# A hybrid mixer layer on one core: the first branch's operand is split beside the query projections, its passes ride in every latent attention pair, and the gate rows' chain is cut into pieces

## The chip, the core and the metric

The kernel runs on one core of a Trainium2 chip. The metric is the device time of that core in microseconds (us). TensorE (PE) multiplies, its weight loads (PEld) overlap its matmuls, VectorE (DVE) and ScalarE (ACT) work through their own programs in order, SyncE (SP) issues the transfers. GpSimd does next to nothing here.

## The reference, cut to what matters

One trunk layer is run for 128 context tokens and 512 latent tokens with the same weights: a half-step SwiGLU FFN, a token mixer, a second FFN. Shapes: D_MODEL 1024, 8 mLSTM heads (64 x 128), 16 query heads over 4 key heads of 64, 128 cached keys.

```python
mq, mk, mv, mo, mg, aq, ak, av, bg = jnp.split(h @ w_in, idx, axis=-1)
hm, C, n, m = mlstm_bidir(mq, mk, mv, mg, C0, n0, m0)     # gates mg: log i, log f, both directions
hm = rms_norm(hm, m_norm) * sigmoid(mo)                   # first branch's operand
ha = block_attention(aq, k_all, v_all)                    # second branch's operand
g = jax.nn.sigmoid(bg.reshape(B, T, 2, D_MODEL))
y = g[:, :, 0] * (hm @ w_bm) + g[:, :, 1] * (ha @ w_ba)
return y @ w_out
```

Context queries see the 128 context keys alone; latent queries see 512 latent and 128 cached keys in one softmax. Everything is float32.

## The kernel before, in words

Activations lie feature-major: 8 chunks of 128 features by 640 tokens (128 context, then 512 latent). A projection tile is 128 output features. Its weights (128 x 1024) are split by ACT into a rounded high part (`whi`, `split` at L850) and by DVE into the rest (`wlo`, L1178); the activations are split in the same way (`_hi`, `_lo`). A tile is 8 chunks x 2 halves of 320 tokens x 3 products (hi*hi, hi*lo, lo*hi): 48 matmuls, 24 for each half (`project`, L446 to 464). Splits run two tiles ahead of PE: `split(t.plus(2))`, into two slots.

Every engine has its own program; the order of work is written out by hand, and semaphores tie the programs together. The mixer's tiles are numbered l: L_GATE (0), four L_MQ (1 to 4), four L_MK (5 to 8), eight L_MV, then output gates and branch gates, L_AV, L_AK, eight L_AQ (queries), and the projections L_BM (first branch), L_BA (second branch) and L_OUT.

Three places are touched.

1. The gate rows. Tile 0 gives 8-partition rows of the gates (`gi`, `gf`). DVE and ACT turn them into stabilised log sums: `forget` (L1392), ACT's Exp and Ln (L992, L994), DVE's `scans` (a step, ten cumulative sums, four maximum scans, small copies, four row operations; L1394 to L1430), ACT's four exponentials (L997 to L1000), then PE's `turn_gates` (transposes and small products, L605, L608) and DVE's `take_gates`. Before the change, DVE runs `forget` at l = 0 and all of `scans` at l = 1, behind the split of tile 3 and ahead of the split of tile 4; ACT's four exponentials stand at l = L_MK - 1 and PE's `turn_gates` behind tile L_MK, where each later tile is followed by one `turn` (a transpose of an earlier tile).

2. The first branch's operand. `out_gate` (L1550) multiplies `hm` by its gate, one chunk for each query tile. The split of `hm` is ACT's `high` (L1109) and DVE's `low_m` (L1614). Both stand in the first eight attention pairs.

3. The attention pairs. A pair is one block of 128 queries for two heads. There are 32 latent pairs (block c >= 1, 640 keys) and 8 context pairs (c = 0, 128 keys). `ORDER` lists them: eight latent pairs, and then eight groups of three latent pairs and one context pair. For pair k, PE runs the scores of pair k + 1 (L756, L759; L751 for context), the transposes of pair k's probabilities (`turn_p`, L775), from the ninth pair on one `fill`, and `values` (L785). A `fill` is a quarter of an L_BM tile, 12 matmuls (L805 to L807); 32 of them do the eight tiles. DVE runs for pair k the two row maxima (`top`, L1585, ahead of the next exponentials), `take_second` of pair k - 1 (L1599, L1602: copies that `values` waits for), the two divisions, `low_ha` (L1609), and behind them what belongs to the fills: `take_fill` (L1624) and a weight split. ACT runs `take_p`, the exponentials of pair k + 1 (L1104), `high_ha` (L1096), and behind them `high`, a gate's Tanh or a weight split.

PE's order for one pair is this:

```python
for k in range(PAIRS):
    if k + 1 < PAIRS:
        scores(k + 1)
    turn_p(k)
    if k >= KC:
        fill(k - KC)
    values(k)
```

The scores of pair k + 1 wait for both exponentials of pair k (`aexp`), the transposes of pair k for `low_ha` of pair k - 1, and the maxima of pair k + 1 for its scores.

Of the kernel before, what the change touches and what calls it, by code (L numbers as in the profile page):

```python
# [21 lines left out]
P = 128  # L22
# [69 lines left out]
def build(nc, a):  # L92
    ctx = ExitStack()
    with ctx:
# [95 lines left out]
        m_hi = at("m_hi", [P, KC, N], F32R, r2)  # L190
# [255 lines left out]
        def _(pe):  # L446
# [343 lines left out]
            def fill(f):  # L790
# [35 lines left out]
            for m in range(KC):  # L826
                gemm(L_OUT + m, h_hi, h_lo, yl if m == 0 else None)
# [16 lines left out]
        def _(act):  # L844
# [28 lines left out]
            def square_y(l, m, t):  # L873
# [4 lines left out]
                fn(sq[m % 2][:, :], y[:, m, :], ACT.Square).then_inc(ysq_in, 1)  # L878
                act.wait_ge(ysq_in, KC * (l + 1) + m + 1)
                for g, cols in GROUPS:  # L880
                    last = fn(y[:, m, cols], y[:, m, cols], ACT.Copy, scale=post_s[:, l, m, g:g + 1])
# [87 lines left out]
            for l in range(L_MO):  # L969
# [20 lines left out]
                else:  # L990
# [4 lines left out]
                if l == L_MK - 1:  # L995
# [59 lines left out]

            def inv_rms(e):
# [7 lines left out]
            for l in range(L_AV, L_BM):  # L1064
# [17 lines left out]
                if l > L_AK:  # L1082
                    inv_rms(l - 1 - L_AK)

# [22 lines left out]
            def high(k, dst, src, ready, count, out):  # L1107
                act.wait_ge(ready, count)
                copy(dst[:, k, :], src).then_inc(out, 1)  # L1109

# [3 lines left out]

            exponentials(0, 0)
# [3 lines left out]
            for k in range(PAIRS):  # L1119
# [5 lines left out]
                if k < KC:  # L1125
                    high(k, h_hi, hm[:, k, :], mg, k + 1, mg_hi)
                elif k % 4 == 0:
                    gate_of(KC + (k - KC) // 4)
                elif k % 4 == 3:
                    split(Tile(T_MIX + L_BM + (k - KC) // 4 + 2))  # L1130

            for l in range(L_BA, L_OUT):
# [5 lines left out]
                if m >= 1:  # L1138
                    high(m - 1, h_hi, y[:, m - 1, :], y_sum, m, yh)
            act.preload_act_table_set(LN_EXP)  # L1140
            high(KC - 1, h_hi, y[:, KC - 1, :], y_sum, KC, yh)

            for l in range(L_OUT, L_END):
# [4 lines left out]
                copy(halves(y[:, m, :]), both(t.slot)).then_inc(ev[t.slot], 1)  # L1148
# [18 lines left out]
        def _(dve):  # L1167
# [42 lines left out]
            def residual(l):  # L1210
# [3 lines left out]
                for k in range(KC):  # L1214
# [3 lines left out]
                    tt(sa[k % 2][:, :], y[:, k, :], rb[:, :], ALU.mult).then_inc(post_t, 1)  # L1218
# [175 lines left out]
            def scans():  # L1394
                dve.wait_ge(row_a, 2)
                row_step(stt(gf[:, :, :], gf[:, :, :], 0.0, t1[:, :, :], ALU.min, ALU.subtract))
                for c in range(NT):
                    for d in range(2):
                        seg = slice(c * P, (c + 1) * P) if d == 0 else slice((c + 1) * P - 1, c * P - 1 if c else None, -1)
                        row_step(dve.tensor_tensor_scan(gb[:, d, seg], one_row, gf[:, d, seg], 0.0, ALU.mult, ALU.add), False)  # L1400
                for d in range(2):
                    for g, cols in GROUPS:
                        if d:
                            cols = slice(cols.stop - 1, cols.start - 1 if cols.start else None, -1)
                        row_step(dve.tensor_tensor_scan(gm[:, d, cols], gf[:, d, cols], gi[:, d, cols],
                                                        m0[:, d:d + 1] if g else 0.0, ALU.add, ALU.max), False)
                dve.wait_ge(row_d, rows[0])
                row_step(dve.memset(m_in[:, :, 0:1], 0.0), False)
                row_step(copy(m_in[:, 0, 1:2], m0[:, 0:1]), False)
                row_step(copy(m_in[:, 1, NT - 1:NT], m0[:, 1:2]), False)  # L1410
                row_step(copy(m_in[:, 0, 2:NT], gm[:, 0, 2 * P - 1:(NT - 1) * P:P]), False)
                row_step(copy(m_in[:, 1, 1:NT - 1], gm[:, 1, 2 * P:(NT - 1) * P + 1:P]), False)
                row_step(copy(mout[:, 0:1], gm[:, 0, TP - 1:TP]), False)
                row_step(copy(mout[:, 1:2], gm[:, 1, 0:1]), False)
                assert rows[0] == ROW_M
                row_step(tt(gi[:, :, :], gi[:, :, :], gb[:, :, :], ALU.subtract), False)
                row_step(tt(nm[:, :, :], gb[:, :, :], gm[:, :, :], ALU.subtract))
                row_step(copy(nml[:, 0, :], nm[:, 0, P - 1:N:P]), False)
                row_step(copy(nml[:, 1, :], nm[:, 1, 0:N:P]))

                def tiles(v):
# [359 lines left out]
```

## Time and profile before

| | |
|---|---|
| three runs | 1950.55, 1951.1, 1955.57 us; median 1951.1 |
| the profiled execution | 1955.21 us, span 1953.4 us |
| PE busy | 1844.7 us (94%) |
| PEld / DVE / ACT busy | 1764.6 (90%) / 940.2 (48%) / 651.6 (33%) us |
| mean granted PE clock | 0.977 |
| HBM | 90 GB/s over the span |

The span is what the profiler records from the first to the last instruction; the 1.8 us beside it lie around it. A busy share is an average over the whole span; the places named above make up about 50 us (gate rows) and 225 us (attention pairs) of it. A granted clock of 1.00 is 2.4 GHz, 0.50 is 1.2 GHz.

### The profile page before, as it was taken

The page shows a single profiled execution, that of the slowest core. Times are in us where ns is not written, and L with a number is a line of the kernel's source. Part 1 is how long each engine was busy: PE and PEld are TensorE (multiplying, and loading weights), DVE is VectorE, ACT ScalarE, POOL GpSimd, SP SyncE. Part 2 cuts the span into 40 slices and gives each one's busy share as a digit, 9 for nine tenths or more (in the row PEclk, how much of TensorE's full clock was granted, in tenths as well). Part 3 has the DMA queues.
Part 4 walks back from the last instruction along what each step waited for, and adds up shares of the span by engine and source line. Part 5 has one row for each costly group of instructions (what it writes and reads, how often), then busy time and mean ns, then how long its engine had stood idle before and what let it go on. Part 6 is the DMA issues. An engine that isn't in the chain of part 4 may idle for free.

```text
span 1953.4 us, 31481 instructions
## 1 busy us (share of the span) xinstructions
PE 1844.7 (94%) x12888; PEld 1764.6 (90%) x12888; DVE 940.2 (48%) x1578; ACT 651.6 (33%) x1067; POOL 0.2 (0%) x4
## 2 busy tenths in 40 slices
PE   6999999999978999999999789999979999999996
PEld 6999999999958998899999668889959999999996
DVE  4665465642575224444434787774363222222235
ACT  3422222112354222533334454442463222221233
POOL 0000000000000000000000000000000000000000
PEclk9999999999988999999999899999989999999997
DMA  7454444412431224222332201112302222222221
GB/s 297 147 159 130 139 150 130 151 65 83 140 100 47 64 74 99 84 75 71 89 123 73 87 2 54 36 36 83 130 33 67 75 74 75 75 75 76 73 57 54
DMA packets 52294, 178.38 MB, mean 91 GB/s; under 512 B 8521, under 2 KB 11099, under 8 KB 51427
## 3 DMA queue, kind: packets, MB, share of 16 engines
q1 hardware_dynamic: 52195, 176.97, 28.1%
q8 instruction: 72, 1.18, 0.2%
q14 instruction: 27, 0.22, 0.0%
HBM read 162.40 MB, written 13.90 MB: 90 GB/s over the span
## 4 chain that ended last, share of the span: by engine, by line
PE 83%; DVE 9%; ACT 4%; issue 3%; DMA 0%; SPq 0%; DVEq 0%; ACTq 0%
PE psum L461 23%; PE psum L462 22%; PE psum L463 22%; PE psum L785 2%; PE psum L503 2%; DVE amax L1585 1%; PE psum L775 1%; PE psum L492 1%; PE psum L756 1%; PE psum L675 1%; DVE x L1213 1%; PE psum L648 1%; DVE macc L1242 1%; DVE wlo L1178 1%; ACT whi L850 1%
## 5 line engine op out<-in xcount | busy, mean ns | idle before, releaser
L461 PE MATMUL psum<-h_hi,whi 128*128 128x320 f32 x2288 | 719.0, 314 | 9.0 <-DVE wlo L1178 7.5
L462 PE MATMUL psum<-h_lo,whi 128*128 128x320 f32 x2288 | 708.9, 310 | 0.0
L463 PE MATMUL psum<-h_hi,wlo 128*128 128x320 f32 x2288 | 708.8, 310 | 0.0
L1178 DVE TENSOR_TENSOR wlo<-raw,whi 128x1024 fp32r<-128x1024 f32 x213 | 260.7, 1225 | 799.7 <-ACT whi L850 798.6
L461 PEld LDWEIGHTS psum<-h_hi,whi 128*128 128x128 f32 x2288 | 431.7, 189 | 15.6 <-DVE wlo L1178 7.8
L462 PEld LDWEIGHTS psum<-h_lo,whi 128*128 128x128 f32 x2288 | 431.8, 189 | 1.9 <-issue 1.9
L463 PEld LDWEIGHTS psum<-h_hi,wlo 128*128 128x128 f32 x2288 | 431.4, 189 | 0.0
L850 ACT CAST whi<-raw 128x1024 fp32r<-128x1024 f32 x213 | 222.3, 1044 | 380.3 <-PE psum L463 370.1
L461 PE MATMUL psum<-g_hi,whi 128*128 128x320 f32 x704 | 218.3, 310 | 1.2 <-DVE g_lo L1307 1.2
L462 PE MATMUL psum<-g_lo,whi 128*128 128x320 f32 x704 | 217.6, 309 | 0.0
L463 PE MATMUL psum<-g_hi,wlo 128*128 128x320 f32 x704 | 217.5, 309 | 0.0
L1242 DVE SCALAR_TENSOR_TENSOR macc<-mw,silc,macc 128x512 f32<-128x512 f32 x210 | 142.7, 744 | 0.0
L461 PEld LDWEIGHTS psum<-g_hi,whi 128*128 128x128 f32 x704 | 132.3, 188 | 1.7 <-DVE g_lo L1307 1.7
L462 PEld LDWEIGHTS psum<-g_lo,whi 128*128 128x128 f32 x704 | 132.3, 188 | 0.0
L463 PEld LDWEIGHTS psum<-g_hi,wlo 128*128 128x128 f32 x704 | 132.3, 188 | 0.0
L928 ACT ACTIVATE sa<-psum 128x640 f32<-128x640 f32 x44 | 31.0, 705 | 151.4 <-PE psum L463 148.4
L785 PE MATMUL psum<-sb,av 128*64 128x128 f32 x672 | 46.6, 282 | 20.5 <-DVE sb L1602 20.4
L785 PEld LDWEIGHTS psum<-sb,av 128*64 128x64 f32 x672 | 37.3, 139 | 28.9 <-issue 28.9
L934 ACT CAST g_hi<-sb 128x640 f32 x44 | 32.1, 729 | 93.2 <-DVE sb L1301 93.2
L1104 ACT ACTIVATE sa<-psum,amax 128x640 f32<-128x640 f32 (+1 forms) x80 | 56.1, 709 | 12.3 <-DVE amax L1585 12.3
L1585 DVE TENSOR_REDUCE amax<-psum 128x1 f32<-128x640 f32 (+1 forms) x80 | 53.5, 710 | 11.2 <-PE psum L759 11.1
L1307 DVE TENSOR_TENSOR g_lo<-sb,g_hi 128x640 f32 x44 | 36.2, 823 | 36.8 <-ACT g_hi L934 36.8
(218 smaller groups left out, 1978.2 us busy)
## 6 DMA issues: line engine op xcount, KB each, us to landing
raw<-in_w_ffn_in SPq DMA_DIRECT2D x88, 512.0 KB, 3.5
raw<-in_w_mix SPq DMA_DIRECT2D x77, 512.0 KB, 3.8
mw<-in_w_mod SPq DMA_DIRECT2D x28, 768.0 KB, 4.7
raw<-in_w_ffn_out SPq DMA_DIRECT2D x32, 512.0 KB, 3.6
mw<-in_w_mod SPq DMA_DIRECT2D x4, 2048.0 KB, 19.6
gate<-gate_keep SPq DMA_DIRECT2D x24, 320.0 KB, 4.9
mw<-in_w_mod SPq DMA_DIRECT2D x14, 512.0 KB, 3.6
gate_keep<-gate SPq DMA_DIRECT2D x20, 320.0 KB, 4.6
```

Of the source, the lines that this page charges most:

```text
L461: mm(out, whi[t.slot][:, k, :], hi[:, k, cols], start=(k == 0), stop=False)
L462: mm(out, whi[t.slot][:, k, :], lo[:, k, cols], start=False, stop=False)
L463: last = mm(out, wlo[t.slot][:, k, :], hi[:, k, cols], start=False, stop=(k == nk - 1))
L503: last = mm(mod_out(2 * t + g, bank), macc[:, g, t * P:(t + 1) * P], ones_d, start=True, stop=True)
L785: last = mm(psum[s * HD:(s + 1) * HD, T_LAST, 2 * P:3 * P], av[:, v, (m // 2) * HD:(m // 2 + 1) * HD], sb[s][:, b * P:(b + 1) * P], start= ...
L850: copy(whi[t.slot][:, :, :], raw[t.raw][:, :, :]).then_inc(w_hi, 1)
L934: copy(out, sb[s][:, :]).then_inc(g_hi_s, 1)
L1104: fn(sa[s][:, 0:w], flat(s)[:, 0:w], ACT.Exp, bias=amax[:, s:s + 1], accum_out=asum[:, s:s + 1]).then_inc(aexp, 1)
L1178: tt(wlo[t.slot][:, :, :], raw[t.raw][:, :, :], whi[t.slot][:, :, :].bitcast(F32), ALU.subtract).then_inc(raw_free, 1)
L1242: last = stt(acc, w[:, k, :], by, acc, ALU.mult, ALU.add)
L1307: tt(g_lo[:, jj, :].rearrange("p o n -> p (o n)"), sb[s][:, :], g_hi[:, jj, :].rearrange("p o n -> p (o n)").bitcast(F32), ALU.subtract).t ...
L1585: dve.tensor_reduce(amax[:, s:s + 1], flat(s)[:, 0:w], AX.X, ALU.max, negate=True).then_inc(nmx, 1)
```

## The change

- The gate rows: `forget` moves to l = 1 and ACT's Exp and Ln with it, behind that tile's copy and split. `scans` gets a part number: the first step and the ten sums at l = 2, the maximum scans and small copies at l = 3, the row operations at l = 4, each behind its tile's weight split. ACT's four exponentials, `turn_gates` and `take_gates` move one tile later (L_MK, L_MK + 1). The `turn` that stood behind tile L_MK + 1 now goes behind L_MK + 2, which has two.
- The operand: `high` and `low_m` write new tiles `a_hi` and `a_lo` (`a_lo` lies where `hm` lies) and run during the query tiles, one chunk for each, one and two tiles behind `out_gate`. What is left of them is `high` of the last chunk ahead of ACT's first exponentials, `low_m` of the last but one behind DVE's query tiles, and `low_m` of the last in pair 0. `m_hi` moves to where `h_hi` lies, and a new `yg` to where `h_lo` lies; it takes the branch sum and the output that `y` had in the mixer.
- The pairs: `ORDER` becomes eight groups of four latent pairs and one context pair. `FILL` gives each latent pair one fill and the context pairs none. DVE takes a half of a fill's tile in the iteration behind the fill; the fourth fill's half and the weight split fall in the iteration of the context pair. ACT's Tanh stands behind the second fill and its split behind the fourth. The last `take_fill` and split, which stood behind the loop, are gone from there.

```diff
-ORDER = [(1, m) for m in range(KC)]
+ORDER, FILL = [], []
 for i in range(KC):
-    ORDER += [(2 + n // KC, n % KC) for n in range(3 * i, 3 * i + 3)] + [(0, i)]
+    ORDER += [(1 + n // KC, n % KC) for n in range(4 * i, 4 * i + 4)] + [(0, i)]
+    FILL += [4 * i, 4 * i + 1, 4 * i + 2, 4 * i + 3, None]
...
-        m_hi = at("m_hi", [P, KC, N], F32R, r2)
+        a_hi = at("a_hi", [P, KC, N], F32R, r2)
+        a_lo = at("a_lo", [P, KC, N], F32R, r1)
+        m_hi = at("m_hi", [P, KC, N], F32R, h_at)
+        yg = at("yg", [P, KC, N], F32, h_at + KC * row)
...
-                if l == L_MK:
+                if l == L_MK + 1:
                     turn_gates()
-                if l > L_MK:
+                if l == L_MK + 2:
+                    turn(0)
+                if l >= L_MK + 2:
                     turn(l - L_MK - 1)
...
-                    mm(out, whi[t.slot][:, k, :], h_hi[:, k, cols], start=(k == 0), stop=False)
-                    mm(out, whi[t.slot][:, k, :], h_lo[:, k, cols], start=False, stop=False)
-                    last = mm(out, wlo[t.slot][:, k, :], h_hi[:, k, cols], start=False, stop=(k == KC - 1))
+                    mm(out, whi[t.slot][:, k, :], a_hi[:, k, cols], start=(k == 0), stop=False)
...
-                if k >= KC:
-                    fill(k - KC)
+                if FILL[k] is not None:
+                    fill(FILL[k])
...
             for m in range(KC):
                 gemm(L_BA + m, m_hi, m_lo)
             for m in range(KC):
-                gemm(L_OUT + m, h_hi, h_lo, yl if m == 0 else None)
+                gemm(L_OUT + m, a_hi, a_lo, yl if m == 0 else None)
...
                 if l > L_GATE:
                     split(t.plus(2))
-                else:
+                if l == L_GATE + 1:
                     act.wait_ge(row_d, 1)
...
-                if l == L_MK - 1:
+                if l == L_MK:
                     act.wait_ge(row_d, ROW_END)
...
+                if l > L_AQ:
+                    m = l - 1 - L_AQ
+                    high(m, a_hi, hm[:, m, :], mg, m + 1, mg_hi)
...
+            high(KC - 1, a_hi, hm[:, KC - 1, :], mg, KC, mg_hi)
             exponentials(0, 0)
...
-                if k < KC:
-                    high(k, h_hi, hm[:, k, :], mg, k + 1, mg_hi)
-                elif k % 4 == 0:
-                    gate_of(KC + (k - KC) // 4)
-                elif k % 4 == 3:
-                    split(Tile(T_MIX + L_BM + (k - KC) // 4 + 2))
+                f = FILL[k]
+                if f is not None and f % 4 == 1:
+                    gate_of(KC + f // 4)
+                if f is not None and f % 4 == 3:
+                    split(Tile(T_MIX + L_BM + f // 4 + 2))
...
-            def scans():
-                dve.wait_ge(row_a, 2)
...
+            def scans(part):
+                if part == 0:
+                    dve.wait_ge(row_a, 2)
+                    row_step(stt(gf[:, :, :], gf[:, :, :], 0.0, t1[:, :, :], ALU.min, ALU.subtract))
+                    for c in range(NT):
+                        for d in range(2):
...
+                elif part == 1:
                     for d in range(2):
-                        seg = slice(c * P, (c + 1) * P) if d == 0 else slice((c + 1) * P - 1, c * P - 1 if c else None, -1)
...
+                    assert rows[0] == ROW_M
+                else:
+                    row_step(tt(gi[:, :, :], gi[:, :, :], gb[:, :, :], ALU.subtract), False)
+                    row_step(tt(nm[:, :, :], gb[:, :, :], gm[:, :, :], ALU.subtract))
...
                 if l == 0:
                     dve.wait_ge(tile_done, 2 + T_MIX)
                     dve.memset(vt[:, :, :, DV:DV + 1], 1.0).then_inc(ones_v, 1)
+                if l == 1:
                     forget()
-                if l == 1:
-                    scans()
-                if l == L_MK:
+                if l in (2, 3, 4):
+                    scans(l - 2)
+                if l == L_MK + 1:
                     take_gates()
-                if l > L_MK:
+                if l == L_MK + 2:
+                    take_turned(0)
+                if l >= L_MK + 2:
                     take_turned(l - L_MK - 1)
...
+            def low_m(m):
+                dve.wait_ge(mg_hi, m + 1)
+                tt(a_lo[:, m, :], hm[:, m, :], a_hi[:, m, :].bitcast(F32), ALU.subtract).then_inc(mg_lo, 1)
...
+                if l > L_AQ + 1:
+                    low_m(l - 2 - L_AQ)
+            low_m(KC - 2)
...
-                if 1 <= k <= KC:
-                    low_m(k - 1)
-                if k > KC and k % 2 == 0:
-                    f = k - KC - 1
+                if k == 0:
+                    low_m(KC - 1)
+                f = FILL[k - 1] if k else None
+                if f is not None and f % 2:
                     take_fill(f // 4, f // 2 % 2)
                     if f % 4 == 3:
                         split(Tile(T_MIX + L_BM + f // 4 + 2))
             take_second(PAIRS - 1)
             low_ha(PAIRS - 1)
-            take_fill(KC - 1, 1)
-            split(Tile(T_MIX + L_BA + 1))
...
-                tt(y[:, m, :], y[:, m, :], sb[m % 2][:, :], ALU.add).then_inc(y_sum, 1)
+                tt(yg[:, m, :], yg[:, m, :], sb[m % 2][:, :], ALU.add).then_inc(y_sum, 1)
```

## Rows read from the trace of the kernel before

**Rows 1.** Page, part 4: shares of the chain that ended last, by engine

```profile
PE 83%; DVE 9%; ACT 4%; issue 3%; DMA 0%; SPq 0%; DVEq 0%; ACTq 0%
```

**Rows 2.** Waits of PE: place, releaser, us in total, times, longest

```profile
PE psum L785 <- DVE sb L1602: 20.4, 15, 1.9
...
PE psum L461 <- DVE wlo L1178: 7.5, 1, 7.5
```

**Rows 3.** Timeline of DVE, gate rows: start us, us, engine, line, operation

```profile
612.80 1.47 DVE L1416 TENSOR_TENSOR gi<-gi,gb 8x1280 f32<-8x1280 f32 x1
...
618.86 2.34 DVE L1178 TENSOR_TENSOR wlo<-raw,whi 128x1024 fp32r<-128x1024 f32 x2
```

**Rows 4.** Timeline of ACT: tile 4's copy, last of the four exponentials

```profile
630.23 0.70 ACT L979 ACTIVATE mq<-psum 128x640 f32<-128x640 f32 x1 [15.95 <-PE psum L463]
...
634.20 1.25 ACT L1000 ACTIVATE gm<-gm 8x1280 f32<-8x1280 f32 x1
```

**Rows 5.** Windows: busy us of PE, PEld, DVE, ACT, POOL; PEclk, DMA share, GB/s

```profile
981.00:983.70 2.70, 0.34 (x4) 0.10 (x2) 2.47 (x7) 0.06 (x1) 0.00 (x0) 1.00 0.11 26
984.80:988.00 3.20, 3.20 (x17) 2.98 (x14) 1.80 (x7) 1.01 (x4) 0.00 (x0) 0.50 0.48 166
...
1100.70:1111.00 10.30, 7.39 (x44) 6.15 (x45) 7.13 (x17) 4.24 (x8) 0.00 (x0) 0.50 0.24 93
1111.00:1153.00 42.00, 29.43 (x315) 25.31 (x315) 35.84 (x81) 23.49 (x53) 0.00 (x0) 1.00 0.00 1
...
620.10:626.30 6.20, 6.18 (x23) 6.19 (x24) 1.10 (x1) 0.00 (x0) 0.00 (x0) 0.50 0.50 169
626.30:630.00 3.70, 3.70 (x27) 3.70 (x26) 0.00 (x0) 0.00 (x0) 0.00 (x0) 1.00 0.00 0
```

**Rows 6.** Timelines of ACT and DVE, last query tile: idle before, releaser, in brackets

```profile
1089.38 0.79 ACT L1074 ACTIVATE aq<-psum,vT 128x640 f32<-128x640 f32 x1 [5.17 <-PE psum L463]
...
1091.74 1.23 DVE L1178 TENSOR_TENSOR wlo<-raw,whi 128x1024 fp32r<-128x1024 f32 x1 [4.22 <-ACT whi L850]
```

**Rows 7.** Timeline of DVE: a chunk's low part and the next maxima

```profile
1127.22 0.82 DVE L1614 TENSOR_TENSOR h_lo<-hm,h_hi 128x640 fp32r<-128x640 f32 x1 [0.32 <-ACT h_hi L1109]
...
1127.96 1.55 DVE L1585 TENSOR_REDUCE amax<-psum 128x1 f32<-128x640 f32 x2
```

**Rows 8.** Timeline of PE: pair 0, then values of two unfilled pairs

```profile
1102.34 2.37 PE L775 MATMUL psum<-cst,sa 128*128 128x128 f32 x10 [1.78 <-DVE sa L1592]
1105.97 2.40 PE L785 MATMUL psum<-sb,av 128*64 128x128 f32 x20 [1.27 <-DVE sb L1602]
...
1124.95 1.31 PE L785 MATMUL psum<-sb,av 128*64 128x128 f32 x20 [1.86 <-DVE sb L1602]
...
1130.65 1.31 PE L785 MATMUL psum<-sb,av 128*64 128x128 f32 x20 [1.86 <-DVE sb L1602]
```

**Rows 9.** Timeline of PE, one group of four: the values of its pairs

```profile
1216.63 1.31 PE L785 MATMUL psum<-sb,av 128*64 128x128 f32 x20 [0.94 <-DVE sb L1602]
...
1222.15 1.31 PE L785 MATMUL psum<-sb,av 128*64 128x128 f32 x20
...
1227.17 1.31 PE L785 MATMUL psum<-sb,av 128*64 128x128 f32 x20
...
1229.70 0.44 PE L775 MATMUL psum<-cst,sa 128*128 128x128 f32 x2
...
1231.82 0.44 PE L785 MATMUL psum<-sb,av 128*64 128x128 f32 x4
```

**Rows 10.** Timeline of DVE in the same group, around the context pair

```profile
1228.85 0.29 DVE L1609 SCALAR_TENSOR_TENSOR m_lo<-psum,m_hi 128x128 fp32r<-128x128 f32 x1 [1.46 <-ACT m_hi L1096]
...
1233.24 0.48 DVE L1624 SCALAR_TENSOR_TENSOR y<-gate,psum 128x320 f32<-128x320 f32 x1
...
1233.87 1.23 DVE L1178 TENSOR_TENSOR wlo<-raw,whi 128x1024 fp32r<-128x1024 f32 x1
```

**Rows 11.** The chain of work: values of the next group's first pair

```profile
1237.69 1.31 PE psum L785 x20
```

More of the change, by code:

```diff
@@ L804, in fill @@
                 for k in range(4 * part, 4 * part + 4):
-                    mm(out, whi[t.slot][:, k, :], h_hi[:, k, cols], start=(k == 0), stop=False)
-                    mm(out, whi[t.slot][:, k, :], h_lo[:, k, cols], start=False, stop=False)
-                    last = mm(out, wlo[t.slot][:, k, :], h_hi[:, k, cols], start=False, stop=(k == KC - 1))
+                    mm(out, whi[t.slot][:, k, :], a_hi[:, k, cols], start=(k == 0), stop=False)
+                    mm(out, whi[t.slot][:, k, :], a_lo[:, k, cols], start=False, stop=False)
+                    last = mm(out, wlo[t.slot][:, k, :], a_hi[:, k, cols], start=False, stop=(k == KC - 1))
                 if part == 1:
@@ L1054, in _, with high @@
             store_hm(UNITS - 2)
+            def high(k, dst, src, ready, count, out):
+                act.wait_ge(ready, count)
+                copy(dst[:, k, :], src).then_inc(out, 1)
             def inv_rms(e):
@@ L1147, in _ @@
                 act.wait_ge(yl, m + 1)
[L1148 removed]
+                copy(halves(yg[:, m, :]), both(t.slot)).then_inc(ev[t.slot], 1)
                 if l == L_END - 1:
@@ L1392, in forget @@
                 row_step(stt(t1[:, :, :], gf[:, :, :], -1.0, gf[:, :, :], ALU.mult, ALU.max))
-            def scans():
-                dve.wait_ge(row_a, 2)
-                row_step(stt(gf[:, :, :], gf[:, :, :], 0.0, t1[:, :, :], ALU.min, ALU.subtract))
-                for c in range(NT):
-                    for d in range(2):
-                        seg = slice(c * P, (c + 1) * P) if d == 0 else slice((c + 1) * P - 1, c * P - 1 if c else None, -1)
[L1400 to L1421, printed above, removed]
-                    return v[:, :, :].rearrange("h d (c t) -> h (d c) t", t=P)
-                def spread(v):
-                    return v[:, :, :].rearrange("h d (c o) -> h (d c) o", o=1).broadcast_to([H, 2 * NT, P])
-                row_step(tt(ar[:, :, :], m_in[:, :, :], nml[:, :, :], ALU.add), False)
-                row_step(tt(tiles(t1), tiles(nm), spread(m_in), ALU.add), False)
-                row_step(tt(tiles(gf), tiles(gi), spread(nml), ALU.add), False)
-                assert rows[0] == ROW_END
@@ new lines, in tiles, with spread @@
+            def tiles(v):
+                return v[:, :, :].rearrange("h d (c t) -> h (d c) t", t=P)
+            def spread(v):
+                return v[:, :, :].rearrange("h d (c o) -> h (d c) o", o=1).broadcast_to([H, 2 * NT, P])
+            def scans(part):
[4 more added lines that the diff above has]
+                        for d in range(2):
+                            seg = slice(c * P, (c + 1) * P) if d == 0 else slice((c + 1) * P - 1, c * P - 1 if c else None, -1)
+                            row_step(dve.tensor_tensor_scan(gb[:, d, seg], one_row, gf[:, d, seg], 0.0, ALU.mult, ALU.add), False)
+                elif part == 1:
+                    for d in range(2):
+                        for g, cols in GROUPS:
+                            if d:
+                                cols = slice(cols.stop - 1, cols.start - 1 if cols.start else None, -1)
+                            row_step(dve.tensor_tensor_scan(gm[:, d, cols], gf[:, d, cols], gi[:, d, cols],
+                                                            m0[:, d:d + 1] if g else 0.0, ALU.add, ALU.max), False)
+                    dve.wait_ge(row_d, rows[0])
+                    row_step(dve.memset(m_in[:, :, 0:1], 0.0), False)
+                    row_step(copy(m_in[:, 0, 1:2], m0[:, 0:1]), False)
+                    row_step(copy(m_in[:, 1, NT - 1:NT], m0[:, 1:2]), False)
+                    row_step(copy(m_in[:, 0, 2:NT], gm[:, 0, 2 * P - 1:(NT - 1) * P:P]), False)
+                    row_step(copy(m_in[:, 1, 1:NT - 1], gm[:, 1, 2 * P:(NT - 1) * P + 1:P]), False)
+                    row_step(copy(mout[:, 0:1], gm[:, 0, TP - 1:TP]), False)
+                    row_step(copy(mout[:, 1:2], gm[:, 1, 0:1]), False)
+                    assert rows[0] == ROW_M
+                else:
+                    row_step(tt(gi[:, :, :], gi[:, :, :], gb[:, :, :], ALU.subtract), False)
+                    row_step(tt(nm[:, :, :], gb[:, :, :], gm[:, :, :], ALU.subtract))
+                    row_step(copy(nml[:, 0, :], nm[:, 0, P - 1:N:P]), False)
+                    row_step(copy(nml[:, 1, :], nm[:, 1, 0:N:P]))
+                    row_step(tt(ar[:, :, :], m_in[:, :, :], nml[:, :, :], ALU.add), False)
+                    row_step(tt(tiles(t1), tiles(nm), spread(m_in), ALU.add), False)
+                    row_step(tt(tiles(gf), tiles(gi), spread(nml), ALU.add), False)
+                    assert rows[0] == ROW_END
```

23 lines of the change are left out of this document (9 added, 14 removed).

## The prediction, made before the change was built

> **What bounds the kernel now.** I read the chain of waits first: 83% of what ended last is PE [rows 1]. So a change pays only where PE stands idle or runs at the lower of its two clock levels. The list of PE's waits names the places that this change can reach [rows 2]: 7.5 us once, in front of a projection tile that waits for the low part of its weights (DVE, L1178), and 20.4 us in 15 waits for DVE's copies ahead of `values`. Then I went to the timelines of these stages, and to the windows for the granted clock. The reader is to see two things. DVE runs its program in order, so the weight split of tile 4 stands behind the whole chain of the gate rows and starts only at 618.86 [rows 3]. And in the attention pairs PE is idle 1.86 us in each pair without a fill [rows 8], while the filled latent pairs of a group have at most 0.94 [rows 9].
>
> **The gate rows in pieces.** Removed is the wait of 7.5 us [rows 2]. With it goes a stretch at 1.2 GHz that it left behind: from 620.1 to 626.3 PE was busy throughout at clock 0.50 and started 23 matmuls in 6.2 us; right behind it, at 1.00, it started 27 in 3.7 us [rows 5]. At the second rate the 23 take 3.2 us, so 3.0 us were lost. Together 10.5 us.
>
> Is something late next? A tile costs PE about 7.0 us (tile 4 from 620.1 to its copy at 630.23 is 10.1, less the 3.0 lost [rows 4, 5]). The largest piece is the row operations, 612.80 to 618.86, 6.1 us [rows 3]. Behind the end of a tile come ACT's copy and split (0.7 and about 1.05, the split taken from the gap up to the exponentials), DVE's split 1.2, hence 3.0 with the hand-overs, and then the piece: 9.1 us behind the end of tile 4, or 2.1 behind the end of tile 5. ACT's exponentials follow; copy, split and exponentials took 630.23 to 635.45, 5.2 us, of which the exponentials are some 3.5 [rows 4]. They end 5.6 us behind tile 5, and `turn_gates` is not reached before 7.0. Slack 1.4 us, so no new wait: 0, with up to 4 us if the pieces queue worse than this. `turn_gates` itself only changes place. The two moved turns and the later `o_m` transfer have nobody waiting. I take -10.5; the ends are -7.5 (the clock is low there for another cause) and -12.
>
> **The operand's split in the query tiles.** ACT waits 5.17 us for PE in each query tile, DVE 4.22 us for ACT [rows 6]; one `high` and one `low_m` (0.74 us from start to start [rows 7]) fit in, price 0. At the end the cover is gone: the last two `low_m` stand in DVE's queue ahead of the first row maximum, on which ACT's exponentials and PE's scores wait. 2 x 0.74 = +1.5. The last `low_m` falls in pair 0 and delays its maxima by 0.74, but PE then has a fill in front of `values`. In pair 0 the fill's 12 matmuls at the low clock (6.2/23 = 0.27 us each) are 3.2 us in place of an idle 1.27 [rows 8]: +1.9. Against that, the three steps from 1105.97 to 1124.95 took 19.0 us instead of 3 x 5.70 = 17.1, because the low clock lasted until 1111 [rows 5, 8]; a PE without idle should have the high clock back by the start of `values`: -1.9. Sum of this part +1.5, ends 0 and +4.
>
> **Passes in each latent pair.** Steps are counted from one `values` to the next. Before: eight unfilled pairs of 5.70 [rows 8] and eight groups of 1237.69 - 1216.63 = 21.06 [rows 9, 11]: 214.1 us. After, a group of five:
> - two steps from latent to latent, PE without idle: 5.52 each, and 5.02 for the one whose scores are the short context scores [rows 9];
> - the step into the context pair. It has no fill now, and DVE has `take_fill` and a weight split there, ahead of the next pair's maxima, and only behind these the small copy that the context's `values` need. From `values`: 1.68 to `low_ha`, 0.29, 0.63 for `take_fill` until the split, 1.23 split, 1.55 for two maxima [rows 7, 9, 10], about 0.3 for the copy (as the 0.29 of the other 128-wide operation), less small overlaps: 5.6. Before it was 4.65 [rows 9];
> - the step out of the context pair: 5.87 before, of which 0.94 was idle behind the same DVE split [rows 9, 11]; the split is gone from there: 4.93.
>
> Sum 5.52 + 5.52 + 5.02 + 5.6 + 4.93 = 26.6, eight times 212.8: -1.3 us. So 17 us of idle in the unfilled pairs are filled, and nearly all of it comes back in the context pairs. Ends -4 and +3.
>
> **The clock in the context pairs.** The new idle is in one piece. Behind `values` PE has the next scores and the two small transposes until 1229.70 + 0.44, 2.97 us behind 1227.17 [rows 9]; then nothing until 5.6: 2.6 us idle, 0.44 of `values`, and again a short wait. What does the clock do with this? At 981 PE was idle for 2.4 us (0.34 busy in 2.70), and from 984.8 to 988.0 the clock stood at 0.50, with PE busy throughout. In the unfilled pairs, with 1.86 us idle each, it stayed at 1.00 from 1111 to 1153 [rows 5, 8]. The new idle is beyond the one that cost the clock. One such fall costs 3.2 us at half speed, 1.5 us by the rate above; a long one, as at 620.1, 3.0 us. Seven context pairs have work behind them. The ends are no fall, 0, and seven long ones, 21 us. I take five short ones, since the idle is only a little beyond the nearest row, and the place of a fall varied: +7.5.
>
> The Trainium skill (TensorE: Matmul & The Clock Gate, Part 1) has PE fall to 1.2 GHz once it has been idle for a while. Read strictly, an idleness that `values` interrupts does not count, no context pair would lose the clock, and the sum would lack the 7.5. By that rule this case's trace differs: at 981 the idle stretch was 2.4 us, PE was busy again at once, and the clock fell all the same [rows 5].
>
> **The sum.** -10.5 + 1.5 - 1.3 + 7.5 = -2.8 us. On the profiled execution's own time, 1955.2 (span 1953.4 and 1.8 around it), that is 1952.4. That execution lies 4.1 above the median of the three runs, 1951.1, so the forecast for the median is 1948.3.
>
> **The rivals.**
> - The clock holds in the context pairs. For it: the stretch is broken by `values`, and the unfilled pairs kept the clock with 30% idle. Against it: 2.6 is more than 2.4. Then -10.3: 1940.8.
> - It ends slower, by one mechanism: the idle in front of each context pair's `values` takes the clock all seven times, and for long stretches as at 620.1, at 3.0 each: 21 us against 10.3 gained, +10.7: 1961.8. It decides from a mean of 1.5 us for each of the seven. For it: the low clock at 1100.7 lasted 10.3 us with PE only 72% busy [rows 5]. Against it: behind a context pair come fills without idle, and behind 984.8 it lasted 3.2.
> - The gate rows' wait goes only in half, because the pieces queue behind splits that wait for ACT: 3.7 us stay and the clock still falls. Then -3.8 in place of -10.5: +3.9, 1955.0. Against it: the slack of 1.4 us above.
>
> **How the numbers follow.** Forecast (three to seven falls near 1.5) 0.57, the clock holds 0.25, all long 0.13, half the wait 0.05. The forecast's own range is 1945.3 (three falls) to 1951.3 (seven). The range for 8 in 10 takes in the first rival nearly and the third: 1941 to 1955. About 0.3%, 5.9 us, is what a measurement of this kernel can tell from no change. Faster by more: the first rival, and the part of the forecast with three falls or fewer, 0.25 + 0.13 = 0.38. Slower by more: most of the second rival, some of the third, and spread, 0.16. Within: 0.46.
>
> **What would show it.** In the profile after: no idle of PE ahead of tile 4, `wlo` of tile 4 ready some 4 us early, and clock 1.00 from 613 on until `turn_gates`; the first maximum 1.5 us behind the last `hm` product; every latent step at 5.5 or 5.0; `values` of a context pair with 2.6 us idle in front, released by DVE's copy; clock 0.50 behind most context pairs. Wrong would be a context step under 5 us (then the maxima don't stand behind the split), a clock of 1.00 through the pairs (first rival), or a wait at `turn_gates` for ACT (third).

## The result, and the profile after

Median 1958.2 us (1955.36 to 1959.43, 8 runs), against 1953.3 us for the kernel before on the same chip (1950.33 to 1955.57, 8 runs). The ratio is 1.0026, 95% interval 1.0018 to 1.0035: 4.9 us slower, inside the 0.3% that I had called no change, and outside my range of 1941 to 1955.

| | before | after |
|---|---|---|
| median of the runs, us | 1953.3 | 1958.2 |
| profiled execution, us | 1955.2 | 1957.5 |
| its span, us | 1953.4 | 1955.8 |
| granted clock, mean | 0.977 | 0.973 |
| PE in the chain that ended last | 83% | 87% |
| waits for DVE's copy ahead of `values` | 15, 20.4 us | 8, 20.4 us |

The share of PE in the chain rose and so did the time: the chain now passes through PE where it passed through DVE (9% before, 6% now), and PE itself is busy 8.5 us longer (1853.2 against 1844.7). A larger share of PE is no gain by itself. Here are the chain's shares in part 4 of the page:

```profile
PE 87%; DVE 6%; ACT 4%; issue 2%; DMA 0%; SPq 0%; DVEq 0%; ACTq 0%
```

and PE's waits (place, releaser, us in total, times, longest). The wait for `wlo` of [rows 2] is gone from the list. The 20.4 us for DVE's copy are the same sum in half as many pieces, which are longer, seven of 2.67 and the eighth of 1.72:

```profile
PE psum L791 <- DVE sb L1621: 20.4, 8, 2.7
```

**The gate rows.** DVE's timeline (start, us, engine, line, operation, idle before and its releaser in brackets) now alternates row operations and splits. `wlo` of tile 4 is made at 605.64; before, DVE reached that split at 618.86 [rows 3]:

```profile
605.64 1.23 DVE L1188 TENSOR_TENSOR wlo<-raw,whi 128x1024 fp32r<-128x1024 f32 x1 [4.50 <-ACT whi L856]
606.78 1.47 DVE L1413 SCALAR_TENSOR_TENSOR gf<-gf,t 8x1280 f32<-8x1280 f32 x1
...
619.65 1.23 DVE L1188 TENSOR_TENSOR wlo<-raw,whi 128x1024 fp32r<-128x1024 f32 x1 [2.33 <-ACT whi L856]
620.79 1.47 DVE L1435 TENSOR_TENSOR gi<-gi,gb 8x1280 f32<-8x1280 f32 x1
```

**The pairs.** PE's timeline: the scores of pair 1, then the steps around the second context pair, then the first tile behind the pairs. A step is counted from one `values` (L791) to the next: 5.01 into the last latent pair of the group, 5.64 into the context pair, 6.35 out of it:

```profile
1088.58 1.70 PE L762 MATMUL psum<-ak,aq 64*128 64x256 f32 x8 [4.79 <-ACT sa L1118]
...
1096.81 1.31 PE L791 MATMUL psum<-sb,av 128*64 128x128 f32 x20
...
1136.15 1.31 PE L791 MATMUL psum<-sb,av 128*64 128x128 f32 x20
1141.16 1.31 PE L791 MATMUL psum<-sb,av 128*64 128x128 f32 x20
1143.69 0.44 PE L781 MATMUL psum<-cst,sa 128*128 128x128 f32 x2
1146.80 0.51 PE L791 MATMUL psum<-sb,av 128*64 128x128 f32 x4 [2.67 <-DVE sb L1621]
...
1153.15 1.31 PE L791 MATMUL psum<-sb,av 128*64 128x128 f32 x20
...
1317.53 0.51 PE L465 MATMUL psum<-m_hi,whi 128*128 128x320 f32 x1 [0.69 <-DVE m_lo L1631]
```

The reader is to see the idle of 2.67 in one piece, and what DVE does meanwhile. Its timeline has the weight split and two maxima, and the copy that PE waits for at their end:

```profile
1143.77 1.23 DVE L1188 TENSOR_TENSOR wlo<-raw,whi 128x1024 fp32r<-128x1024 f32 x1 [0.25 <-ACT whi L856]
1144.91 1.54 DVE L1607 TENSOR_REDUCE amax<-psum 128x1 f32<-128x640 f32 x2
1146.37 0.28 DVE L1621 COPY sb<-psum 128x128 f32<-128x128 f32 x1
```

**The clock.** The windows have the columns of [rows 5]; the column behind POOL is the granted clock:

```profile
596.00:640.00 44.00, 44.00 (x309) 43.78 (x308) 23.18 (x38) 16.16 (x18) 0.00 (x0) 0.96 0.23 79
634.00:638.00 4.00, 4.00 (x21) 3.98 (x21) 1.42 (x3) 0.00 (x0) 0.00 (x0) 0.63 0.38 135
1100.00:1318.00 218.00, 193.09 (x1728) 167.68 (x1727) 153.50 (x392) 96.97 (x247) 0.00 (x0) 0.93 0.09 30
1147.00:1149.80 2.80, 2.63 (x16) 1.86 (x12) 1.34 (x4) 0.62 (x3) 0.00 (x0) 0.51 0.50 196
1149.80:1174.00 24.20, 22.10 (x212) 19.48 (x210) 17.73 (x45) 10.87 (x28) 0.00 (x0) 0.99 0.01 2
1174.50:1180.40 5.90, 5.55 (x27) 4.63 (x28) 3.40 (x10) 2.33 (x7) 0.00 (x0) 0.50 0.39 132
1317.30:1320.70 3.40, 3.17 (x12) 3.17 (x13) 0.18 (x1) 0.48 (x1) 0.00 (x0) 0.56 0.62 236
```

Over all eight groups the clock is 0.93, where the long quiet stretch of before had 1.00 [rows 5]. It falls behind every one of the eight context pairs, back to full within the same group. Six of these stretches are about 3.4 us long, and two, at the third and the sixth context pair, about twice that; the one at 1147 is the second, the one of 1174.5 to 1180.4 the third. The eighth lies in the first tile behind the pairs, at 1317.

The chain gives the length of a group. It has the `values` of the fourth latent pair of the first group and of the eighth, seven groups later:

```profile
1112.95 1.27 PE psum L791 x20
...
1312.30 1.27 PE psum L791 x20
```

(1312.30 - 1112.95) / 7 = 28.48 us, where the prediction has 26.6 without falls. That is 1.9 us a group.

### The profile page after: what moved, and what is told of

Same layout as the page of the kernel before. It is cut to its first block, busy times and chain, and to the rows that moved or that the text cites. A ratio compares the mean times of both kernels' runs of the same rounds, so it can differ in the third digit from the quotient of the medians.

```text
span 1955.8 us, 31481 instructions
## 1 busy us (share of the span) xinstructions
PE 1853.2 (95%) x12888; PEld 1771.7 (91%) x12888; DVE 941.0 (48%) x1578; ACT 650.5 (33%) x1067; POOL 0.2 (0%) x4
## 4 chain that ended last, share of the span: by engine, by line
PE 87%; DVE 6%; ACT 4%; issue 2%; DMA 0%; SPq 0%; DVEq 0%; ACTq 0%
PE psum L465 23%; PE psum L467 22%; PE psum L466 22%; PE psum L781 2%; PE psum L791 2%; PE psum L762 2%; PE psum L507 1%; PE psum L496 1%; PE psum L811 1%; PE psum L812 1%; PE psum L813 1%; ACT whi L856 1%; PE psum L681 1%; DVE x L1223 1%; PE psum L654 1%
## 5 line engine op out<-in xcount | busy, mean ns | idle before, releaser
L465 PE MATMUL psum<-h_hi,whi 128*128 128x320 f32 x2160 | 678.1, 314 | 1.5 <-ACT gate L1018 1.5
L466 PE MATMUL psum<-h_lo,whi 128*128 128x320 f32 x2160 | 668.4, 309 | 0.0
L467 PE MATMUL psum<-h_hi,wlo 128*128 128x320 f32 x2160 | 668.3, 309 | 0.0
L465 PEld LDWEIGHTS psum<-h_hi,whi 128*128 128x128 f32 x2160 | 406.5, 188 | 7.8 <-issue 5.4
L466 PEld LDWEIGHTS psum<-h_lo,whi 128*128 128x128 f32 x2160 | 406.7, 188 | 1.9 <-issue 1.9
L467 PEld LDWEIGHTS psum<-h_hi,wlo 128*128 128x128 f32 x2160 | 406.5, 188 | 0.0
L791 PE MATMUL psum<-sb,av 128*64 128x128 f32 x672 | 46.4, 281 | 20.4 <-DVE sb L1621 20.4
L791 PEld LDWEIGHTS psum<-sb,av 128*64 128x64 f32 x672 | 36.4, 138 | 28.3 <-issue 28.3
L1607 DVE TENSOR_REDUCE amax<-psum 128x1 f32<-128x640 f32 (+1 forms) x80 | 53.5, 710 | 16.1 <-PE psum L765 16.1
L781 PE MATMUL psum<-cst,sa 128*128 128x128 f32 x336 | 51.2, 302 | 4.3 <-DVE m_lo L1631 3.0
```

The lines of the kernel that those rows point to most:

```text
L465: mm(out, whi[t.slot][:, k, :], hi[:, k, cols], start=(k == 0), stop=False)
L466: mm(out, whi[t.slot][:, k, :], lo[:, k, cols], start=False, stop=False)
L467: last = mm(out, wlo[t.slot][:, k, :], hi[:, k, cols], start=False, stop=(k == nk - 1))
L781: last = tp(turned(s, b), sa[s][:, b * P:(b + 1) * P], ident)
L791: last = mm(psum[s * HD:(s + 1) * HD, T_LAST, 2 * P:3 * P], av[:, v, (m // 2) * HD:(m // 2 + 1) * HD], sb[s][:, b * P:(b + 1) * P], start= ...
L1607: dve.tensor_reduce(amax[:, s:s + 1], flat(s)[:, 0:w], AX.X, ALU.max, negate=True).then_inc(nmx, 1)
```

## The experiments

All times are medians of four or five runs, each beside the kernel before on the same chip: 1953.1 us for the first four experiments, 1953.5 for the next four, 1952.8 for the last three.

### Each half by itself

The gate rows alone, on the kernel before:

```
 for l in range(2, L_MO):
     gemm(l)
-    if l == L_MK:
+    if l == L_MK + 1:
         turn_gates()
...
-    scans()
+    if l in (2, 3, 4):
+        scans(l - 2)
...
```

> The kernel before with the gate rows alone in pieces. My theory (the gate rows gain what was forecast, and the attention pairs give it back through the clock): 10.5 us faster than before, about 1943, no idle of PE ahead of tile 4. Rival (the pieces gain less than the profile says, because the profiled run of before was a slow one): 3 to 6 us faster.

The pairs alone: the changed kernel, with the gate rows as before.

> The changed kernel with the gate rows as they were before: the operand's split and the passes alone. My theory: about 15 us slower than before, 1968, of which 1.5 is low_m ahead of the first maxima and 13 to 15 the low clock behind eight context pairs. Rival (the two parts interact, for instance through where the clock's falls lie): the sum of this and the rows alone is off the changed kernel's +5 by more than 3 us.

Measured: 1942.5 us (1942.35 to 1943.03), ratio 0.9948 [0.9935, 0.9962], for the rows; 1966.2 us (1964.58 to 1969.37), ratio 1.0070 [1.0056, 1.0083], for the pairs. So -10.6 and +13.1. The sum, +2.5, is 2.4 us off the +4.9 of both together, and each of the two ratios is uncertain by about 2.6 us, so no interaction of the halves can be told. Windows of the rows' kernel: PE has no idle, and the pairs keep the clock.

```profile
596.00:640.00 44.00, 44.00 (x309) 43.78 (x308) 23.18 (x38) 16.20 (x18) 0.00 (x0) 0.96 0.22 74
1098.00:1316.00 218.00, 194.29 (x1826) 171.40 (x1825) 161.61 (x402) 104.38 (x256) 0.00 (x0) 1.00 0.10 34
```

Windows of the pairs' kernel: the same 44 us have 7.5 us of idle again, and the pairs stand at 0.93.

```profile
596.00:640.00 44.00, 36.50 (x253) 36.02 (x252) 21.95 (x37) 15.15 (x17) 0.00 (x0) 0.92 0.19 61
1108.00:1327.00 219.00, 194.10 (x1739) 168.56 (x1736) 154.03 (x392) 96.84 (x247) 0.00 (x0) 0.93 0.09 29
```

The prediction's first term, -10.5, holds. The error is in the pairs, which with the operand's split were forecast at +7.7.

### The idle filled with work that nobody reads

If the pairs cost because the clock falls, then extra matmuls in the idle should make the kernel faster:

```
 if FILL[k] is not None:
     fill(FILL[k])
+else:
+    for n in range(NWARM):      # NWARM = 24
+        mm(psum[:, T_LAST, 3 * P:4 * P], a_hi[:, n % KC, 0:P], a_hi[:, n % KC, 0:P], start=True, stop=True)
 values(k)
```

> The changed kernel with 24 extra 128-column matmuls in each context pair, between its transposes and its values, into a free quarter of a PSUM bank (nothing reads them): work added, in PE's idle 2.7 us. If the clock is the cause: clock 1.00 through the pairs, steps out of a context pair back at 4.9 us, 12 to 15 us faster than the changed kernel, about 1944. If the loss is the wait itself (DVE's chain) and the clock only goes along: the same time as the changed kernel, or up to 3 us slower.

Measured: 1944.0 us (1943.31 to 1946.11), ratio 0.9957 [0.9944, 0.9971], 14.2 us under the changed kernel. The window over the pairs, with 274 more matmul records in the same 218 us (192 of them the added ones), stands at 1.00:

```profile
1100.00:1318.00 218.00, 212.46 (x2002) 190.65 (x2001) 155.62 (x395) 98.15 (x249) 0.00 (x0) 1.00 0.10 35
```

PE's timeline of one group. The 24 matmuls take 2.88 us of the old idle, and the step out of the context pair is 1229.93 - 1224.97 = 4.96, where the changed kernel has 6.35:

```profile
1203.27 1.31 PE L792 MATMUL psum<-sb,av 128*64 128x128 f32 x20
...
1219.34 1.31 PE L792 MATMUL psum<-sb,av 128*64 128x128 f32 x20
1222.06 2.88 PE L831 MATMUL psum<-a_hi 128*128 128x128 f32 x24
1224.97 0.44 PE L792 MATMUL psum<-sb,av 128*64 128x128 f32 x4
...
1229.93 1.31 PE L792 MATMUL psum<-sb,av 128*64 128x128 f32 x20
```

The group is 1229.93 - 1203.27 = 26.66, the prediction's 26.6. So the steps were right, and 14.2 us is the price of the falls: shown, since the only change was added work. The rival, that the wait itself costs the time and the clock only goes along, is out: the step into the context pair is as long as before (1224.97 - 1219.34 = 5.63), and the 14.2 us are gone.

### The idle made shorter: the split one pair later

```
 if f is not None and f % 2:
     take_fill(f // 4, f // 2 % 2)
-    if f % 4 == 3:
-        split(Tile(T_MIX + L_BM + f // 4 + 2))
+f = FILL[k - 2] if k >= 2 else None
+if f is not None and f % 4 == 3:
+    split(Tile(T_MIX + L_BM + f // 4 + 2))
...
 low_ha(PAIRS - 1)
+split(Tile(T_MIX + L_BA + 1))
```

> The changed kernel with one thing moved: DVE's weight split stands one iteration later, behind the first latent pair of the next group. Theory: the context pair's values then wait only about 1.5 us, the step into it is 4.5 us in place of 5.6, no fall of the clock; 5 us of steps and 13 to 15 us of clock: 18 to 20 us faster than the changed kernel, about 1939, and faster than before. Rival (the split only shifts the idle into the next step, whose maxima it then delays): the idle and the falls move there, the time stays within 3 us of the changed kernel.

Measured: 1944.3 us (1942.04 to 1944.44), ratio 0.9952 [0.9939, 0.9966]. It is 13.9 under the changed kernel, but 5 us over what I expected, and this is the miss that taught most. The idle in front of the context pair's `values` is 1.58 us now (0.55 at the eighth), less than the 1.86 of the unfilled pairs that kept the clock [rows 8]. PE's timeline, at the first, the fifth and the eighth context pair:

```profile
1116.95 0.44 PE L791 MATMUL psum<-sb,av 128*64 128x128 f32 x4 [1.58 <-DVE sb L1621]
...
1219.93 1.31 PE L791 MATMUL psum<-sb,av 128*64 128x128 f32 x20
...
1224.47 0.44 PE L791 MATMUL psum<-sb,av 128*64 128x128 f32 x4 [1.58 <-DVE sb L1621]
...
1303.21 0.44 PE L791 MATMUL psum<-sb,av 128*64 128x128 f32 x4 [0.55 <-DVE sb L1621]
```

The step is 4.54 in place of 5.64. But the clock still falls, behind the second to the sixth context pair and behind the eighth; behind the first and the seventh, with the same 1.58 us of idle, it holds. The windows of this kernel: over all pairs 0.95, behind the first context pair full speed, behind the second half speed with PE busy throughout:

```profile
1100.00:1318.00 218.00, 200.49 (x1804) 177.00 (x1803) 155.22 (x394) 98.17 (x249) 0.00 (x0) 0.95 0.10 34
...
1117.40:1122.30 4.90, 4.36 (x35) 3.91 (x35) 4.81 (x12) 2.59 (x8) 0.00 (x0) 1.00 0.32 95
...
1144.20:1147.60 3.40, 3.40 (x21) 3.01 (x17) 2.97 (x5) 0.74 (x2) 0.00 (x0) 0.50 0.27 72
```

The 1.1 us that the step into the context pair lost came back in part: the moved split makes the step out of it 5.34 with 0.31 idle where the clock holds, against 4.96 before. That leaves 0.7 us for each of seven groups and 1.2 at the eighth, about 6 of the 13.9 us. The rest is in the falls: six short ones are left, at about 1.2 us each (a step out of 6.55 in place of 5.34), of the six short and two long ones. The length of PE's idle by itself doesn't tell whether the clock falls.

### The same with twelve idle matmuls

> The kernel with DVE's split one iteration later, and 12 extra 128-column matmuls in each context pair's remaining idle of 1.6 us (nothing reads them). The run with the split moved alone lost the clock behind seven of eight context pairs although its idle is shorter than the 1.86 us that the unfilled pairs of before had. Theory (the idle's length alone was the wrong measure: the small products of a context pair count for little, and real work in the gap keeps the clock): no fall in the pairs, 8 to 11 us faster than with the split moved alone, about 1935. Rival (the clock falls for the wait as such, whatever is put in): the falls stay, 1944.

The expectation counts seven falls in the kernel before this one; its profile has six. The edit is the two above together, with `NWARM = 12`. Measured: 1937.9 us (1937.28 to 1939.32), ratio 0.9919 [0.9905, 0.9932], 6.5 us under the kernel without them, where I had expected 8 to 11. The window:

```profile
1110.00:1300.00 190.00, 181.22 (x1742) 160.06 (x1738) 143.61 (x371) 91.19 (x233) 0.00 (x0) 1.00 0.09 33
```

No fall is left, and six falls cost 6.5 us, 1.1 each. The rival, that the clock falls for the wait as such, whatever is put into it, is out.

### The order of before, with the rest of the change

```
-    ORDER += [(1 + n // KC, n % KC) for n in range(4 * i, 4 * i + 4)] + [(0, i)]
-    FILL += [4 * i, 4 * i + 1, 4 * i + 2, 4 * i + 3, None]
+    ORDER += [(2 + n // KC, n % KC) for n in range(3 * i, 3 * i + 3)] + [(0, i)]
+FILL = [None] * KC + list(range(4 * KC))
...
 low_ha(PAIRS - 1)
+take_fill(KC - 1, 1)
+split(Tile(T_MIX + L_BA + 1))
```

> The changed kernel with ORDER and the fills as they were before: gate rows in pieces and the operand's split in the query tiles, but eight unfilled pairs first. It tells the two parts of the attention change apart. Theory (the order alone brings the loss; the moved split is worth 8 x 0.36 us in the unfilled pairs less 1.5 at their start): 1 to 2 us faster than the gate rows alone, about 1941, no falls in the pairs. Rival (the moved split is part of the loss, by delaying the start or by other falls): 3 us or more slower than the gate rows alone.

Measured: 1941.9 us (1941.15 to 1944.05), ratio 0.9941 [0.9927, 0.9955]. The kernel with the gate rows alone has the ratio 0.9948, so the operand's split in the query tiles, which is all that is between the two, makes no difference that can be told. The window of the pairs is at full clock:

```profile
1110.00:1300.00 190.00, 172.59 (x1652) 151.15 (x1648) 144.05 (x368) 90.90 (x231) 0.00 (x0) 1.00 0.10 33
```

The loss is thus in the order of the pairs and their fills.

### A part of the tile in the context pair

The same four parts of a tile, one of them moved from a latent pair into the context pair. The last `take_fill` and split stand behind the loop again, since the last fill now stands in the last pair:

```
-    FILL += [4 * i, 4 * i + 1, 4 * i + 2, 4 * i + 3, None]
+    FILL += [4 * i, 4 * i + 1, 4 * i + 2, None, 4 * i + 3]
...
 low_ha(PAIRS - 1)
+take_fill(KC - 1, 1)
+split(Tile(T_MIX + L_BA + 1))
```

> The changed kernel with the fourth quarter of each tile moved from the fourth latent pair into the context pair, so that a latent pair is without a fill instead (its scores are the short context ones). The split and take_fill then fall behind the next group's first pair, as before the change. Theory: the work of 1.95 us covers the context pair's wait and keeps the clock; steps 5.5, 5.5, about 4.3, 4.65, 5.9, 25.9 a group against 28.3 with the falls: 14 to 20 us faster than the changed kernel, about 1940. Rival (the idle then stands in the unfilled latent pair and takes the clock there): within 5 us of the changed kernel.

Measured: 1941.1 us (1938.68 to 1941.38), ratio 0.9933 [0.9920, 0.9947], 17.2 us under the changed kernel by one changed list, as expected. PE's timeline, with an idle of 1.27 now in front of a latent pair:

```profile
1190.26 1.31 PE L791 MATMUL psum<-sb,av 128*64 128x128 f32 x20 [1.27 <-DVE sb L1624]
```

The clock holds there too, so the rival, that the falls move with the idle, is out. The window:

```profile
1110.00:1300.00 190.00, 169.15 (x1625) 147.41 (x1623) 142.96 (x367) 91.01 (x233) 0.00 (x0) 1.00 0.10 33
```

### The tile in five parts

No pair without a fill: the 48 matmuls of a tile in parts of 12, 12, 9, 9 and 6.

```
-    FILL += [4 * i, 4 * i + 1, 4 * i + 2, 4 * i + 3, None]
+    FILL += [(i, 0, 0, 4), (i, 0, 4, 8), (i, 1, 0, 3), (i, 1, 3, 6), (i, 1, 6, 8)]
...
-                for k in range(4 * part, 4 * part + 4):
+                for k in range(lo, hi):
...
```

> The changed kernel with each L_BM tile cut into five parts of 12, 12, 9, 9 and 6 matmuls, one for every pair of a group, the context pair too; take_fill and the split of a tile fall behind the next group's first pair. Theory: no pair is without projection work, so the clock stays; steps 5.5, 5.5, 5.3, 4.6, about 4.7, 5.9: 25.6 to 26.2 a group, 16 to 20 us faster than the changed kernel, about 1940. Rival (6 matmuls, 0.9 us, are too little work for the clock): falls behind most context pairs as with the split moved alone, about 1946.

Measured: 1937.5 us (1936.35 to 1938.67), ratio 0.9916 [0.9903, 0.9930]. PE's timeline, a context pair and the latent pair behind it; the two longest idles of a group are 0.70 and 0.95:

```profile
1196.20 0.44 PE L791 MATMUL psum<-sb,av 128*64 128x128 f32 x4 [0.70 <-DVE sb L1621]
...
1202.18 1.31 PE L791 MATMUL psum<-sb,av 128*64 128x128 f32 x20 [0.95 <-DVE sb L1624]
```

Its window shows the full clock:

```profile
1110.00:1300.00 190.00, 171.78 (x1644) 149.24 (x1639) 143.93 (x372) 90.90 (x234) 0.00 (x0) 1.00 0.10 33
```

### Five parts and the split one pair later

The last part is done in the context pair, so DVE's weight split falls into the step behind it. The edit is that of the later split, on top of the five parts.

> The five-part kernel with DVE's weight split one iteration later still, behind the second latent pair. In the five-part kernel the step out of a context pair is 5.98 us with 0.95 idle, because take_fill and the split stand ahead of the next maxima. Theory: that wait shrinks to about 0.3 and the split's 1.2 us fit mostly behind a step that PE bounds: 0.4 to 0.7 us a group, 3 to 5 us faster, about 1934. Rival (the split then delays the maxima of the second step by as much): 1937, no change.

Measured: 1932.0 us (1931.38 to 1933.18, 4 runs), ratio 0.9895 [0.9880, 0.9910]. That is 5.5 us under the five parts alone, a little more than the 3 to 5 expected. The step out of the context pair is 1199.18 - 1194.22 = 4.96, without idle, where it was 5.98; the step behind it took 0.2 of this back (5.70 in place of 5.52):

```profile
1194.22 0.44 PE L791 MATMUL psum<-sb,av 128*64 128x128 f32 x4 [0.70 <-DVE sb L1621]
1199.18 1.31 PE L791 MATMUL psum<-sb,av 128*64 128x128 f32 x20
```

### The two low parts behind the first maxima

The 1.5 us that I had put on the two `low_m` ahead of the first row maximum:

```
-    if l > L_AQ + 1:
+    if L_AQ + 1 < l < L_BM - 1:
         low_m(l - 2 - L_AQ)
-low_m(KC - 2)
...
+    low_m(KC - 3)
     turn_halves(QK - 1)
...
 if k == 0:
+    low_m(KC - 2)
     low_m(KC - 1)
```

> The five-part kernel with the two low_m that stood ahead of the first maxima moved behind them: one ahead of the last key rotation, one behind pair 0's divisions. It prices the +1.5 us of the forecast by itself. Theory: the first exponentials start 1.5 us earlier, and 1.0 to 1.5 us of it reach the end: 1936.3, with the first maxima directly behind the last product with hm. Rival (pair 0's copies are then late by as much): no change, 1937.5.

And with the later split:

> Both of these together. If they are independent, the sum of the two: 1932 to 1934, the fastest of all kernels here. If either only shifts a wait, the better of the two.

Measured: 1937.9 us (1934.40 to 1938.77), ratio 0.9922 [0.9908, 0.9935], against 0.9916 for five parts alone: nothing that the medians can tell, where I had expected 1.0 to 1.5 us. PE's wait for the first exponentials is back from 4.79 to 3.31. PE's timelines, from the last rotation of the queries (L717), the kernel in five parts first, then the one with the low parts behind:

```profile
1083.13 1.31 PE L717 MATMUL psum<-sq,cst 128*128 128x320 f32 x4 [1.14 <-DVE sb L1577]
...
1090.09 2.08 PE L762 MATMUL psum<-ak,aq 64*128 64x256 f32 x8 [4.79 <-ACT sa L1118]
...
1098.11 1.31 PE L791 MATMUL psum<-sb,av 128*64 128x128 f32 x20
```

```profile
1083.99 1.31 PE L717 MATMUL psum<-sq,cst 128*128 128x320 f32 x4 [1.14 <-DVE sb L1577]
...
1089.47 1.13 PE L762 MATMUL psum<-ak,aq 64*128 64x256 f32 x8 [3.31 <-ACT sa L1118]
...
1098.26 1.31 PE L791 MATMUL psum<-sb,av 128*64 128x128 f32 x20
```

The two executions reach the rotation at different times, so the distance from it counts: the first `values` stand 14.98 us behind it in the first and 14.27 in the second. Of the 1.5 us, 0.7 arrive. The rest went in two places behind the scores: PE waits 1.95 us for DVE's divisions ahead of the turn of pair 0, where it waited 0.99, and then the fill lies deeper in the stretch of low clock that both kernels have here (to 1098.1 in place of 1096.9). A gain of 0.7 us is within the spread of these runs. The kernel with both edits measured 1930.7 us (1930.34 to 1931.95, 4 runs), ratio 0.9891 [0.9876, 0.9906]: the fastest of all, a little under the 1932 to 1934 expected, 22.1 us under the kernel before and 27.5 under the changed one, but not to be told from the 1932.0 without this edit.

## Why the prediction was wrong

It was wrong by one term, the clock's price. The forecast was -2.8 us and +4.9 was measured; the other 2.2 us between 1948.3 and 1958.2 are its base, which was the median of three runs of the kernel before (1951.1), where eight gave 1953.3. By its own steps, in the two profiled executions:

**The gate rows, -10.5: right.** From the start of tile 2 to the scores of pair 1 the kernel after is 8.9 us shorter, which holds the 1.5 that the two `low_m` add. The experiment with this half alone gives -10.6. No wait took its place, and the 1.4 us of slack at `turn_gates` held: PE is busy 44.00 of 44 us.

**The operand's split, +1.5: right in sum.** PE's wait for the first exponentials went from 3.31 to 4.79 us. Of the rest, `values` of pair 0 stand 1.5 us farther behind the scores (I had 1.9), and the next three steps take 1112.88 - 1096.81 = 16.1 us, at full clock, in place of 19.0, which holds the forecast 1.9 of low clock. Together +1.1.

**The steps, 26.6 a group: right.** Predicted 5.52, 5.52, 5.02, 5.6 and 4.93; measured 5.52, 5.52, 5.01 and 5.64 in the changed kernel and 4.96 where the clock holds; a group of 26.66.

**The clock, "I take five short ones, since the idle is only a little beyond the nearest row": this step failed, in count and in size.** All eight context pairs lost the clock, two of them for about twice as long, which a forecast of equal short falls leaves out. By the step out of the context pair, 4.96 at full clock, a short fall cost 1.2 to 1.6 us and a long one 2.6 (steps of 6.19 to 6.59, and 7.54 and 7.62). The seven groups are 1.87 us each over 26.6, hence 13.1, and the eighth fall adds 1.6 behind the pairs: 14.7 in place of 7.5. I had also said that seven context pairs have work behind them. The eighth has too: its low stretch slows the first tile behind the pairs.

With 14.7 the sum is -10.5 + 1.5 - 1.3 + 14.7 = +4.4. The spans differ by +2.4, since 1.7 us were gained before tile 2, where nothing was changed: the execution of before has a stretch of half clock at 523.8 to 527.2 that the one of after lacks, with PE busy in both. From tile 2 on it is +4.1, so the sum closes to 0.3. The first rival had the clock's price at 0, the second at 21. The mechanism of the second rival is what acted, at 1.8 a fall and eight times, where it had 3.0 and seven times; its point of decision, 1.5 for each of seven, was passed, and the change ended slower, by 0.25%.

**The rule weighed.** Read strictly, the Trainium skill (TensorE: Matmul & The Clock Gate, Part 1) would have no fall, since `values` breaks the idle. The traces differ eight times out of eight. And my own yardstick, the length of the longest idle beside that of one earlier fall, failed in the same way: 1.86 us per pair kept the clock from 1111 to 1153 in the kernel before [rows 5, 8], and when the split was moved 1.58 us cost it in five of the seven context pairs that have it, and 0.55 at the eighth.

What I should have seen ahead: the neighbours of the idle. In the unfilled pairs the idle lies among full scores, turns and values. In the context pair there are full scores, but 2 turns in place of 10 and 4 `values` matmuls in place of 20. The five parts, which put a fill there, keep the clock from the first `values` to the last. That the neighbours decide is argued from these cases, not shown by a run that changes them alone, and they can't be all of it: the seven context pairs with 1.58 us of idle have the same work around it, and two of them kept the clock. What sets these two apart is open, and so is what makes a fall long.

## What to carry to other kernels

Spread filler work so that the poorest stretch gets some, before filling every rich one: one changed list, with the same matmuls, was worth 17 us of 1958. A gap costs more than its own length if the clock falls behind it, and then each such fall returns at the loop's period, so multiply by all passes, the last too. Ask of an operation in order on DVE, such as a split for a later tile, whether it can stand one pair later: in the two versions with five parts that was worth 5.5 us (1937.5 to 1932.0) and 7.2 (1937.9 to 1930.7).

## What the runs showed of the hardware

- Idle work can pay: 24 extra matmuls of 128 columns in each context pair, 2.88 us of PE that nobody reads, made the kernel 14.2 us faster. In the stream each took 120 ns.
- The clock fell behind 1.58 us of idle among short work in five context pairs of seven, and held with 1.86 us in every pair of 5.70 [rows 8]. No single length of idle in these traces separates the two, and the same sequence of work did both.
- It fell also without any idle: `turn_gates`, 38 matmuls of 8 and 10 columns in a row, runs from 632.0 to 634.8, and in the 4.00 us from 634 on PE was busy 4.00 us at a granted clock of 0.63. The 44 us that hold it stand at 0.96 for that reason, and not at 1.00.
- One recurring fall cost 1.1 us (six falls, 6.5 us) to 1.9 us (the mean of seven groups of the changed kernel, two long ones of 2.6 among them).
